# The sample stage of a two-layer hybrid decoder step: earlier first fills, scores one block later, one activation between two evictions

## The chip, the cores and the metric

The kernel runs on one core of one Trainium2 chip. The metric is the device time of one execution in microseconds (us), lower is better. A core has a TensorE (PE: matmuls, and transposes done as matmuls with the identity), a VectorE (DVE), a ScalarE (ACT), a GpSimd (POOL) and a SyncE (SP) that issues DMAs. Each engine works through its own instructions in order and waits on semaphores that the others raise. Matmuls write to PSUM, which has 8 banks of 512 fp32 per partition; DVE and ACT read it. Copying a bank to SBUF is called an eviction here.

## The reference, cut to what matters

One inference step of a prompt (512 tokens) and of 8 samples (4 tokens each, 2048 tokens of past in paged caches): one mLSTM layer, a shared K/V projection, one layer of native sparse attention. The change touches the attention of the samples alone. Per sample it computes, in fp32:

```python
sub = rows.reshape(M, 16, 2, HKV, HD)                      # raw cache rows, M = 128 blocks of 16 tokens
first  = einsum('mpchd,cpde->mche', sub, cmp_w1[:, :16])   # c = 0 keys, 1 values
second = einsum('mpchd,cpde->mche', sub, cmp_w1[:, 16:])
hid = silu(first[:-1] + second[1:] + cmp_b1)               # (127, 2, 4, 128)
out = einsum('mche,ced->mchd', hid, cmp_w2)                # compressed keys (norm + rotary) and values
p_c = softmax(q @ kc);  o_c = p_c @ vc                     # compressed branch
score = p_c summed over heads and overlapping blocks, + forced blocks; the 16 best of 33 are kept
o_s = softmax(q @ k_sel, others hidden) @ v_sel            # selected branch, over all 2048 rows with a mask
o_w = softmax(q @ k_win) @ v_win                           # window branch, 512 rows
y = g0*o_c + g1*o_s + g2*o_w
```

## The kernel before, in words

The program has six stages one after another, with barriers between them: inputs, mLSTM, projections, prompt attention, sample attention (`phase_sample`, lines 1929 to 2474) and output. Only `phase_sample` is touched. In the profile it lies from 1664 us to 2149 us.

It handles the 8 samples in a software pipeline of two. `attend(seg, n, with_next)` does the attention of sample n; between its steps PE does `products` of sample n+1, the first layer of the compression. The seven passes of the loop (`pe.Fori(0, NS - 1)`, n = 0 to 6) each hold one sample's attention and the next sample's products. Sample 0's products come ahead of the loop, and sample 7's attention comes behind it with nothing in between.

- **Fills.** Each sample takes 30 "fills", numbered 0 to 29: PE writes one bank (mostly by four transposes), and ACT or DVE evicts it. Fill j goes to bank j % 3. Fills 0 to 7 turn the cached rows for the products of c = 0 (`turn_pieces`, L2102), 8 and 9 the window keys and 11 to 18 the selected keys (`turn_keys`, L2131), 10 holds window scores, 19 to 26 turn the rows for c = 1, and 27 to 29 turn the probabilities (L2212 to L2219). `FILLS_ON_ACT` says which are evicted by ACT (0, 2, 4, 6, 8, 9, 11, ...), the others by DVE. `room(seg, j)` is PE's wait before a fill: for the eviction of fill j - 3, which had the same bank, if that is in the same run of fills; for the first three of a run it waits by another rule (line 2089).
- **Runs.** `Fills` counts a segment's fills, so that a wait can be written as a number of evictions. Inside the loop a segment is all of 0 to 29. Ahead of the loop it is 0 to 7 and 19 to 26 (two runs); for the last sample 8 to 18 and 27 to 29.
- **Products.** `products(seg, c, ks)` (L2112) is two matmuls for each block k; `fill_in(c, [k])` does them for the next sample inside `attend`. They sum in bank 3 (c = 0) and bank 7 (c = 1). `hid_mm` counts finished sums, and ACT's `silu` (L2283) reads the bank and raises `hid_ok`, for which the second layer (L2153) at the head of `attend` waits.
- **Scores.** `score(seg, 0)` and `score(seg, 1)` (L2139) multiply queries with four slots of turned keys each, so they wait for the evictions of fills 11 to 14 and 15 to 18. `oc_mm` (L2205) is the compressed branch's output, `top_in` says that DVE has read the block scores out of bank 4.
- **The other engines.** ACT's order is written out in its own `attend` and in the loop at L2326, DVE's likewise. POOL gathers the paged rows by indirect DMA and copies them to `pieces`: the selected rows of sample n+1 are asked for once `pv_mm` (L2241) of sample n is done. SP loads the window rows and, near the end, the output weights.

Inside the loop PE goes through: fills 0 to 7, second layer, block 0 of c = 0, fills 8 and 9, block 1, fill 10, blocks 2 and 3, fills 11 to 14, compressed scores (L2182), score 0, block 4, transpose of the compressed probabilities (L2187), fills 15 to 18 with small matmuls between them (L2190, L2195), score 1, blocks 5 to 7, fills 19 to 26, blocks 0 and 1 of c = 1, `oc_mm`, fills 27 to 29, blocks 2 and 3, `pv_mm`, blocks 4 to 7.

Of the kernel before, what the change touches and what calls it, by code (L numbers as in the profile page):

```python
# [16 lines left out]
ACT = mybir.ActivationFunctionType  # L17
# [5 lines left out]
TP, NS, TS_ = 512, 8, 4  # L23
# [1903 lines left out]
def phase_sample(nc, I, S):  # L1927

    with ExitStack() as ctx:
# [62 lines left out]
        def both(n):  # L1992
            return Fills(range(30), n * 30 + n_front, n * on_act + n_front // 2, n * (30 - on_act) + n_front // 2)
# [85 lines left out]
        def _(pe):  # L2079
            ident = C("ident")  # L2080

            def room(seg, j):

                if j - 3 in seg.fills:
                    if j - 3 in FILLS_ON_ACT:
                        pe.wait_ge(E["out_a"], seg.out_a(j - 3))
                    else:
                        pe.wait_ge(E["out_d"], seg.out_d(j - 3))
                elif seg is not first[0] or j >= 3:
                    pe.wait_ge(E["out_a"], seg.out_a(j - 1))  # L2090
                    pe.wait_ge(E["out_d"], seg.out_d(j - 1))

# [49 lines left out]
            def attend(seg, n, with_next):  # L2142


                def fill_in(c, ks):
                    if with_next:
                        products(seg, c, ks)
# [33 lines left out]
                for pr in range(2):  # L2181
                    t = pe.matmul(bank[strip(0, pr), 4, 0:M - 1], qz[:, pr, :], kct[:, pr, :], start=True, stop=True)  # L2182
                t.then_inc(E["cs_mm"], 1)
                score(seg, 0)
                fill_in(0, [4])
                hold(pe, E["cs_ok"], n + 1, E["pass_pe"])
# [7 lines left out]
                for half in range(2):  # L2194
                    t = pe.matmul(bank[half * R:(half + 1) * R, 4, 0:NSEL], C("same_ht"), ov[:, :], start=True, stop=True)  # L2195
                t.then_inc(E["group_mm"], 1)
                score(seg, 1)
                fill_in(0, [5, 6, 7])
                if with_next:
                    turn_pieces(seg, n + 1, 1)  # L2200
                fill_in(1, [0, 1])

                pe.wait_ge(E["top_in"], n + 1)
# [3 lines left out]
                t.then_inc(E["oc_mm"], 1)  # L2207

                hold(pe, E["exp_ok"], n * 2 + 2, E["pass_pe"])
# [53 lines left out]
        def _(act):  # L2263

            def pieces_out(seg, m, c):
                for j in (range(0, 8, 2) if c == 0 else range(19, 27, 2)):
                    act.wait_ge(E["turned"], seg.turned(j))
                    if j == 19:
                        act.wait_ge(E["hid_mm"], m * 2 + 1)
                    if j == 0 and seg is not first[0]:  # L2270
                        act.wait_ge(E["hid_mm"], m * 2)
                    out, src = xt_of(j)
                    act.copy(out, src).then_inc(E["out_a"], 1)
# [5 lines left out]

            def silu(m):  # L2280
                for c in range(2):
                    act.wait_ge(E["hid_mm"], m * 2 + c + 1)
                    act.activation(hid[:, c, :, :], bank[:, 3 if c == 0 else 7, 0:BKV * (M - 1)].rearrange("p (h m) -> p h m", h=BKV),  # L2283
                                   ACT.Silu, bias=S.b1[:, c:c + 1]).then_inc(E["hid_ok"], 1)

            def attend(seg, n, with_next):
# [23 lines left out]
                if with_next:  # L2310
                    pieces_out(seg, n + 1, 1)
                act.wait_ge(E["max_ok"], n * 2 + 2)
# [9 lines left out]

            pieces_out(first[0], 0, 0)
            pieces_out(first[0], 0, 1)
            silu(0)
            with act.Fori(0, NS - 1) as n:  # L2326
                pieces_out(both(n), n + 1, 0)
                attend(both(n), n, True)
                silu(n + 1)
            attend(last, NS - 1, False)  # L2330
# [318 lines left out]
```

## Time and profile before

| | |
|---|---|
| median of 3 runs | 2231.38 us (2228.94 to 2234.61) |
| the profiled execution's own time | 2226.32 us |
| its span, first to last instruction | 2224.7 us |
| PE busy | 2019.6 us (91% of the span) |
| DVE, ACT, POOL busy | 702.8, 473.8, 226.5 us |
| mean granted TensorE clock | 0.946 |

The profile shows one execution. A timeline row gives the start, the duration, engine, line, operation and tile of a group of instructions that follow each other, and in brackets how long the engine sat idle before it and what released it. Matmul ends are modelled and matmuls overlap, so a group's start is more certain than its end, and the time from one group's start to the next one's start says what a step really takes. PE counts each fp32 matmul twice. A row of waits sums the idle time of one line by releaser, with the number of times and the longest. A row of windows gives the busy time of each engine in a stretch, the clock granted to TensorE there (1.00 is its upper level, 2.4 GHz; 0.50 would be the lower, 1.2 GHz), and the DMA share.

### The profile page before, as it was taken

To read this page: it belongs to the slowest core of one execution; us is meant where nothing else is said; L and a number is where in the kernel's file an instruction comes from. 1 tells how busy PE (TensorE), PEld (TensorE's weight loads), DVE (VectorE), ACT (ScalarE), POOL (GpSimd) and SP (SyncE) were. 2 spreads that over 40 slices of the span, in tenths; PEclk is the share of its full clock that TensorE was granted. 3 is DMA by queue.
4 is the path that set the end of the run, shared out by engine and by line. 5 is a ranking of instruction groups with operands and counts; after the bars stand their busy time and mean duration, and the time that the engine had idled before them with its cause. 6 is when DMAs were issued, how large, how long until landed. Compare 5 with 4: busy or idle time off the path is not lost. (4 is left out here: it accounts for less than half of the span.)

```text
span 2224.7 us, 26140 instructions
## 1 busy us (share of the span) xinstructions
PE 2019.6 (91%) x9651; PEld 1177.8 (53%) x9651; DVE 702.8 (32%) x1553; ACT 473.8 (21%) x1028; POOL 226.5 (10%) x332
## 2 busy tenths in 40 slices
PE   6998999999999999978889999578869999999878
PEld 3225554664555466447754468445545555555457
DVE  2011323332332332230121340355542444444332
ACT  1110211121121112110020012244442333333310
POOL 0000010001001000100000000132332111111000
PEclk9998999999999999989999998688889999999979
DMA  6753353246134423623312164400004444443331
GB/s 177 265 202 139 134 179 143 77 167 240 48 122 173 158 77 137 229 90 127 108 44 76 42 157 147 156 2 1 1 18 192 167 163 170 170 170 141 116 94 41
DMA packets 119263, 281.31 MB, mean 126 GB/s; under 512 B 33224, under 2 KB 41870, under 8 KB 115447
## 3 DMA queue, kind: packets, MB, share of 16 engines
q1 hardware_dynamic: 101004, 170.57, 23.3%
q0 software_dynamic: 12928, 109.54, 12.2%
q10 hardware_dynamic: 5268, 0.36, 0.3%
q8 instruction: 40, 0.66, 0.1%
q14 instruction: 23, 0.19, 0.0%
HBM read 227.79 MB, written 60.86 MB: 130 GB/s over the span
## 5 line engine op out<-in xcount | busy, mean ns | idle before, releaser
L2112 PE MATMUL sample_bank<-area 128*128 128x508 f32 x512 | 232.4, 599 | 7.2 <-DVE area L2352 7.2
L1022 DVE SCALAR_TENSOR_TENSOR mlstm_cring<-mlstm_cring,mlstm_cur_old,mlstm_bank 128x512 f32<-128x512 f32 x128 | 87.1, 743 | 223.4 <-PE mlstm_bank L788 223.4
L2112 PEld LDWEIGHTS sample_bank<-area 128*128 128x128 f32 x512 | 92.6, 190 | 116.2 <-issue 106.5
L1302 PE MATMUL proj_bank<-stage,area 128*128 128x512 f32 x320 | 142.9, 605 | 6.3 <-ACT area L1379 6.3
L706 PE MATMUL mlstm_bank<-h,stage 128*128 128x272 f32 x512 | 120.7, 398 | 7.6 <-SPq L594 7.6
L761 PE MATMUL mlstm_bank<-h,stage 128*128 128x272 f32 x512 | 121.2, 395 | 0.0
L772 PE MATMUL mlstm_bank<-stage,h 128*128 128x512 f32 x256 | 114.1, 599 | 0.0
L706 PEld LDWEIGHTS mlstm_bank<-h,stage 128*128 128x128 f32 x512 | 98.5, 193 | 28.3 <-DVEq L941 7.7
L317 PE MATMUL start_bank<-stage,start_c_t 128*9 128x512 f32 x256 | 111.3, 592 | 1.8 <-DMA stage<-in_b_ada_w 0.6
L1731 PE MATMUL prompt_bank<-const,x 128*128 128x128 f32 x336 | 64.5, 337 | 52.4 <-ACT area L1802 42.7
L723 PE MATMUL mlstm_bank<-stage,h 128*128 128x512 f32 x256 | 110.9, 594 | 0.0
L761 PEld LDWEIGHTS mlstm_bank<-h,stage 128*128 128x128 f32 x512 | 96.0, 190 | 27.9 <-issue 9.1
L1302 PEld LDWEIGHTS proj_bank<-stage,area 128*128 128x128 f32 x320 | 61.1, 193 | 87.8 <-issue 86.3
L1678 POOL TENSOR_SCALAR x<-x,prompt_coef,gnat 128x128 f32<-128x128 f32 (+3 forms) x128 | 76.5, 607 | 171.8 <-DVE prompt_coef L1879 171.7
L1731 PEld LDWEIGHTS prompt_bank<-const,x 128*128 128x128 f32 x336 | 46.7, 172 | 86.7 <-POOL x L1678 64.1
L1787 ACT ACTIVATE x<-prompt_bank,prompt_nm 128x128 f32<-128x128 f32 (+3 forms) x128 | 66.3, 524 | 102.7 <-DVEq L1872 98.6
L2102 PE MATMUL sample_bank<-const,sample_pieces 128*128 128x128 f32 x512 | 68.3, 284 | 19.0 <-DVE area L2352 6.7
L2352 DVE COPY area<-sample_bank 128x512 f32<-128x512 f32 x64 | 44.2, 691 | 125.8 <-PE sample_bank L2102 125.8
L772 PEld LDWEIGHTS mlstm_bank<-stage,h 128*128 128x128 f32 x256 | 47.3, 190 | 66.0 <-issue 66.0
L723 PEld LDWEIGHTS mlstm_bank<-stage,h 128*128 128x128 f32 x256 | 48.3, 190 | 62.7 <-issue 62.7
L2102 PEld LDWEIGHTS sample_bank<-const,sample_pieces 128*128 128x128 f32 x512 | 58.4, 145 | 35.9 <-issue 20.1
L1260 PE MATMUL proj_bank<-area,stage 128*128 128x272 f32 x256 | 60.5, 400 | 17.6 <-DMA area<-act_scratch 17.6
(489 smaller groups left out, 2752.4 us busy)
## 6 DMA issues: line engine op xcount, KB each, us to landing
stage<-in_a_w_in SPq DMA_DIRECT2D x16, 2048.0 KB, 9.0
mlstm_cring<-in_state_C SPq DMA_DIRECT2D x32, 1024.0 KB, 5.4
o_Cs<-mlstm_cring POOLq DMA_DIRECT2D x32, 1024.0 KB, 4.7
stage<-in_a_ada_w SPq DMA_DIRECT2D x6, 2048.0 KB, 7.9
stage<-in_b_ada_w SPq DMA_DIRECT2D x6, 2048.0 KB, 8.0
stage<-in_kv_ada_w SPq DMA_DIRECT2D x4, 2048.0 KB, 7.9
stage<-in_a_w_out SPq DMA_DIRECT2D x4, 2048.0 KB, 10.8
sample_winr<-in_cache_kv_win SPq DMA_DIRECT2D x8, 1024.0 KB, 5.2
```

The costliest lines, as they stand in the source:

```text
L317: last = pe.matmul(bank[0:NS + 1, s, :], c_t[:, k, :], ada_w[:, s, k, :], start=(k == 0), stop=(k == KD - 1))
L706: last = pe.matmul(o[:, 0:HALF], win[:, 0, k, i * P:(i + 1) * P], S.h[:, k, at:at + HALF], start=(k == 0), stop=(k == KD - 1))
L723: last = pe.matmul(o, S.h[:, k, i * P:(i + 1) * P], win[:, 1, k, :], start=(k == 0), stop=(k == KD - 1))
L761: last = pe.matmul(o[:, 0:HALF], win[:, 0, k, i * P:(i + 1) * P], S.h[:, k, half * HALF:(half + 1) * HALF], start=(k == 0), stop=(k == KD ...
L772: last = pe.matmul(o, S.h[:, k, i * P:(i + 1) * P], win[:, 1, k, :], start=(k == 0), stop=(k == KD - 1))
L1022: dve.scalar_tensor_tensor(c, c, cur_old[:, n:n + 1], bank[:, b_big("outer", n * KH + k), :], ALU.mult, ALU.add).then_inc(E["c_new"], 1)
L1302: last = pe.matmul(o, h[:, k, a * P:(a + 1) * P], w[:, k, :], start=(k == 0), stop=(k == KD - 1))
L1678: last = pool.tensor_scalar(prob[:, u % 3, h, 0:w], prob[:, u % 3, h, 0:w], coef[:, u % 3, h:h + 1], S.gnat[:, a, at:at + 1], ALU.mult, AL ...
L1731: last = pe.transpose(out[:, b * P:(b + 1) * P], src, ident)
L1787: act.activation(prob[:, u % 3, h, 0:w], sc_bank(u, h)[:, 0:w], ACT.Exp, bias=nm[:, u % 3, h:h + 1], accum_out=den[:, u % 3, h:h + 1])
L2102: t = pe.transpose(bank[:, j % 3, q * M:(q + 1) * M], pieces[:, p % BKV, k * P:(k + 1) * P], ident)
L2112: t = pe.matmul(out, S.w1[:, c, o * 8 + k, :], xt[:, k, :, o:o + M - 1], start=(k == 0 and o == 0), stop=(k == 7 and o == 1))
```

## The change

1. `room`: the first three fills of a run no longer wait for all fills ahead of them, the run's own first ones among them, but for the fills ahead of the run.
2. PE in `attend`: block 4 of c = 0 goes ahead of score 0; block 5 goes ahead of score 1; `oc_mm` goes ahead of blocks 0 and 1 of c = 1.
3. ACT: the second `silu` (c = 1) of a sample goes from the end of a loop pass to the head of the next one, behind the eviction of fill 0 and ahead of those of fills 2, 4 and 6. After the last pass it stands alone behind the loop.

```diff
                 elif seg is not first[0] or j >= 3:
-                    pe.wait_ge(E["out_a"], seg.out_a(j - 1))
-                    pe.wait_ge(E["out_d"], seg.out_d(j - 1))
+                    run = max(f for f in seg.fills if f <= j and f - 1 not in seg.fills)
+                    pe.wait_ge(E["out_a"], seg.out_a(run - 1))
+                    pe.wait_ge(E["out_d"], seg.out_d(run - 1))
...
                 t.then_inc(E["cs_mm"], 1)
+                fill_in(0, [4])
                 score(seg, 0)
-                fill_in(0, [4])
...
                 t.then_inc(E["group_mm"], 1)
+                fill_in(0, [5])
                 score(seg, 1)
-                fill_in(0, [5, 6, 7])
+                fill_in(0, [6, 7])
                 if with_next:
                     turn_pieces(seg, n + 1, 1)
-                fill_in(1, [0, 1])
-
                 pe.wait_ge(E["top_in"], n + 1)
...
                 t.then_inc(E["oc_mm"], 1)
-
+                fill_in(1, [0, 1])
                 hold(pe, E["exp_ok"], n * 2 + 2, E["pass_pe"])
...
-            def silu(m):
-                for c in range(2):
-                    act.wait_ge(E["hid_mm"], m * 2 + c + 1)
+            def silu(m, c):
+                act.wait_ge(E["hid_mm"], m * 2 + c + 1)
...
-            pieces_out(first[0], 0, 0)
-            pieces_out(first[0], 0, 1)
-            silu(0)
+            pieces_out(first[0], 0, (0, 2, 4, 6))
+            pieces_out(first[0], 0, (19, 21, 23, 25))
+            silu(0, 0)
             with act.Fori(0, NS - 1) as n:
-                pieces_out(both(n), n + 1, 0)
+                pieces_out(both(n), n + 1, (0,))
+                silu(n, 1)
+                pieces_out(both(n), n + 1, (2, 4, 6))
                 attend(both(n), n, True)
-                silu(n + 1)
+                silu(n + 1, 0)
+            silu(NS - 1, 1)
             attend(last, NS - 1, False)
```

`pieces_out` on ACT takes its list of fills as an argument now; the lists are the old ones.

On ACT the loop's first instructions are these, as one piece of the difference (`sample_bank` is PSUM, `area` holds the turned rows, `sample_hid` the activated first layer; the semaphores carry names of an earlier stage that used the same ones: `start_x_in` is `hid_mm`, `start_const_in` is `turned`):

```order
 L2271 ISA [waits start_const_in]
 L2273 COPY area<-sample_bank 128x4x128 [waits start_x_in]
+L2281 ISA
+L2282 ACTIVATE sample_hid<-sample_bank,b 128x508 [waits start_x_in]
 L2267 REGISTER_ALU
 L2273 COPY area<-sample_bank 128x4x128 [waits start_const_in]
```

The activation stands behind the eviction of fill 0, which has its two waits as before, and ahead of that of fill 2; no table load comes with it.

On PE, around score 1 (L2139, L2140 in the changed kernel), before:

```order
L2195 MATMUL sample_bank<-x,const 64x33 x2
L2135 REGISTER_ALU
L2136 REGISTER_ALU
L2139 MATMUL sample_bank<-sample_kt,x 32x512 x4
L2112 MATMUL sample_bank<-area 128x508 x6
```

and in the changed kernel:

```order
L2196 MATMUL sample_bank<-x,const 64x33 x2
L2113 MATMUL sample_bank<-area 128x508 x2
L2136 REGISTER_ALU
L2137 REGISTER_ALU
L2140 MATMUL sample_bank<-sample_kt,x 32x512 x4
L2113 MATMUL sample_bank<-area 128x508 x4
```

One block (two matmuls) of the next sample's products moved from behind the score to ahead of it; around score 0 it is the same with block 4.

On PE, behind fills 19 to 26 (L2102, L2103 in the changed kernel), before:

```order
L2102 MATMUL sample_bank<-const,sample_pieces 128x128 x4
L2107 REGISTER_ALU
L2108 REGISTER_ALU
L2112 MATMUL sample_bank<-area 128x508 x4
L2205 MATMUL sample_bank<-x 32x128 x2
```

and in the changed kernel:

```order
L2103 MATMUL sample_bank<-const,sample_pieces 128x128 x4
L2205 MATMUL sample_bank<-x 32x128 x2
L2108 REGISTER_ALU
L2109 REGISTER_ALU
L2113 MATMUL sample_bank<-area 128x508 x4
```

The two small matmuls `oc_mm` moved ahead of the two registers that hold the blocks' wait for the evictions, and of the blocks.

## Rows read from the trace of the kernel before

**Rows 1.** The page: busy time, share of the span, instructions by engine.
```profile
PE 2019.6 (91%) x9651; PEld 1177.8 (53%) x9651; DVE 702.8 (32%) x1553; ACT 473.8 (21%) x1028; POOL 226.5 (10%) x332
```

**Rows 2.** Windows: length, busy us (and count) of PE, PEld, DVE, ACT, POOL; PEclk, DMA, GB/s.
```profile
400.00:500.00 100.00, 99.66 (x421) 63.51 (x420) 30.65 (x66) 19.89 (x41) 6.99 (x13) 1.00 0.34 123
1764.14:1819.80 55.66, 52.06 (x346) 30.32 (x345) 22.59 (x66) 17.98 (x33) 10.30 (x12) 1.00 0.42 170
2124.00:2132.00 8.00, 2.92 (x12) 2.00 (x12) 2.67 (x4) 1.89 (x4) 0.00 (x0) 0.66 0.52 99
```

**Rows 3.** Waits of PE, 1667 to 2140 us: us in total, times, longest.
```profile
PE sample_bank L2139 <- DVE sample_kt L2357: 7.9, 16, 0.6
PE sample_bank L2112 <- DVE area L2352: 7.2, 9, 0.9
PE sample_bank L2102 <- DVE area L2352: 6.7, 7, 1.0
PE sample_bank L2102 <- ACT area L2273: 6.5, 8, 0.9
```

**Rows 4.** Timeline of PE, head of the loop's second pass: fills 0 to 7.
```profile
1764.14 0.60 PE L2102 MATMUL sample_bank<-const,sample_pieces 128*128 128x128 f32 x4
1765.61 0.65 PE L2102 MATMUL sample_bank<-const,sample_pieces 128*128 128x128 f32 x4 [0.86 <-ACT area L2273]
1767.22 3.04 PE L2102 MATMUL sample_bank<-const,sample_pieces 128*128 128x128 f32 x24 [0.96 <-DVE area L2352]
1770.10 1.88 PE L2153 MATMUL sample_bank<-w,sample_hid 128*127 128x64 f32 x16
```

**Rows 5.** Timeline of ACT in the same stretch, and its eviction of fill 19.
```profile
1764.35 0.68 ACT L2283 ACTIVATE sample_hid<-sample_bank,b 128x508 f32<-128x508 f32 x1 [10.73 <-PE sample_bank L2112]
1764.97 0.58 ACT L2273 COPY area<-sample_bank 128x512 f32<-128x512 f32 x1
...
1796.59 0.58 ACT L2273 COPY area<-sample_bank 128x512 f32<-128x512 f32 x1 [7.52 <-PE sample_bank L2102]
```

**Rows 6.** Timeline of PE, same pass: both scores, fills 19 to 26, `oc_mm`.
```profile
1782.54 0.41 PE L2182 MATMUL sample_bank<-x 128*32 128x127 f32 x4
1783.39 1.07 PE L2139 MATMUL sample_bank<-sample_kt,x 128*32 128x512 f32 x8 [0.44 <-DVE sample_kt L2357]
...
1786.29 0.32 PE L2187 MATMUL sample_bank<-const,x 64*127 64x64 f32 x1
...
1788.81 0.31 PE L2195 MATMUL sample_bank<-x,const 64*64 64x33 f32 x4
1789.67 1.07 PE L2139 MATMUL sample_bank<-sample_kt,x 128*32 128x512 f32 x8 [0.55 <-DVE sample_kt L2357]
...
1795.88 3.96 PE L2102 MATMUL sample_bank<-const,sample_pieces 128*128 128x128 f32 x32
1800.63 3.67 PE L2112 MATMUL sample_bank<-area 128*128 128x508 f32 x8 [0.78 <-DVE area L2352]
1804.23 0.41 PE L2205 MATMUL sample_bank<-x 127*32 127x128 f32 x4
```

**Rows 7.** Timeline of DVE, same pass: the step that releases L2187.
```profile
1785.56 0.28 DVE L2391 TENSOR_SCALAR x<-x,sample_denc 64x127 f32<-64x127 f32 x1
```

**Rows 8.** Timeline of PE ahead of the loop: fill 19, and the blocks behind fill 26.
```profile
1688.15 0.60 PE L2102 MATMUL sample_bank<-const,sample_pieces 128*128 128x128 f32 x4
...
1694.73 1.52 PE L2112 MATMUL sample_bank<-area 128*128 128x508 f32 x3 [0.87 <-DVE area L2352]
```

**Rows 9.** Timeline of PE, last sample: fills 28 and 29.
```profile
2129.29 1.12 PE L2219 MATMUL sample_bank<-const,x 128*128 128x128 f32 x4 [0.72 <-ACT x L2317]
2131.28 1.09 PE L2219 MATMUL sample_bank<-const,x 128*128 128x128 f32 x4 [0.87 <-DVE x L2424]
```

**Rows 10.** Timeline of POOL: selected rows asked for; DMA issues: median us to landing.
```profile
1813.88 0.96 POOL L1578 DMA_INDIRECT sample_sel<-in_cache_kv_sel,sample_sblk  x1 [39.20 <-PE sample_bank L2241]
...
sample_sel<-in_cache_kv_sel,sample_sblk POOLq DMA_INDIRECT x8, 14.4
```

More of the change, by code:

```diff
@@ L2263, in _, with pieces_out @@
         def _(act):
-            def pieces_out(seg, m, c):
-                for j in (range(0, 8, 2) if c == 0 else range(19, 27, 2)):
+            def pieces_out(seg, m, fills):
+                for j in fills:
                     act.wait_ge(E["turned"], seg.turned(j))
@@ L2278, in keys_out @@
                 act.copy(out, src).then_inc(E["out_a"], 1)
-            def silu(m):
-                for c in range(2):
-                    act.wait_ge(E["hid_mm"], m * 2 + c + 1)
-                    act.activation(hid[:, c, :, :], bank[:, 3 if c == 0 else 7, 0:BKV * (M - 1)].rearrange("p (h m) -> p h m", h=BKV),
-                                   ACT.Silu, bias=S.b1[:, c:c + 1]).then_inc(E["hid_ok"], 1)
+            def silu(m, c):
+                act.wait_ge(E["hid_mm"], m * 2 + c + 1)
+                act.activation(hid[:, c, :, :], bank[:, 3 if c == 0 else 7, 0:BKV * (M - 1)].rearrange("p (h m) -> p h m", h=BKV),
+                               ACT.Silu, bias=S.b1[:, c:c + 1]).then_inc(E["hid_ok"], 1)
             def attend(seg, n, with_next):
@@ L2310, in attend @@
                 if with_next:
-                    pieces_out(seg, n + 1, 1)
+                    pieces_out(seg, n + 1, (19, 21, 23, 25))
                 act.wait_ge(E["max_ok"], n * 2 + 2)
```

## The prediction
> **What bounds the kernel now.** I read the page first: PE is busy 2019.6 of 2224.7 us [rows 1], so only time that PE loses can be won. The windows then say what the stage in question looks like: one loop pass is 55.7 us, PE is busy for 52.06 of it, ACT for 18 and DVE for 22.6, the DMAs for 0.42, and TensorE's clock is granted in full, 1.00 [rows 2]. So in the loop PE is the bound, and the remaining 3.6 us of a pass are its waits. The list of PE's waits names them: 6.7 and 6.5 us ahead of fills (L2102), 7.9 us ahead of scores (L2139), 7.2 us ahead of blocks (L2112), all for an eviction by DVE or ACT [rows 3]. The times are seven or eight (sixteen for the two scores) with the longest hardly above the mean: the same short waits in each pass. The timelines show where they lie, and the change aims at each of them.
>
> **The first fills of a pass (change 1 with 3).** Fill 0 starts at 1764.14. Fill 1 waits until ACT has evicted fill 0 (idle 0.86), fill 2 until DVE has evicted fill 1 (idle 0.96); the six from fill 2 on then run through, and the second layer starts at 1770.10 [rows 4]. That is 5.96 us from start to start. The bank of fill 1 was free all the while. With the new rule fills 0, 1 and 2 follow each other, and what eight fills then take is shown by fills 19 to 26, which have no such wait today: 3.96 us, or about 3.8 to the next start, since a group's start lies 0.1 to 0.2 ahead of the modelled end of the one before (1770.10 against 1767.22 + 3.04 = 1770.26) [rows 4, 6].
>
> ACT must keep that pace. Today it does the activation (0.68 us from 1764.35) and then evicts fill 0 at 1764.97 [rows 5]. In the run of fills 19 to 26 the first eviction starts 0.71 us after the first fill (1795.88 to 1796.59) [rows 5, 6], so fill 0's should start at 1764.85 and end at 1765.43, and the activation follows until 1766.1. Fill 2, ready at about 1765.7, is then evicted until 1766.7, and fill 5, which needs that bank, starts some 2.6 us behind fill 0, where the undisturbed pace (3.8/8 for each fill, five of them) puts it at 2.4 to 2.5. I charge 0.1. The second layer needs the activation 3.9 us behind fill 0, at 1768.0; it is done by 1766.1, so the moved activation has 1.9 us of cover. The gain is 5.96 - 3.9 = **2.05 us** a pass. Bounds: if the whole activation stood on the path, 2.15 - 0.68 = 1.5; without any disturbance 2.15.
>
> **Score 0 behind block 4.** From the compressed scores (1782.54) to the transpose L2187 (1786.29) PE takes 3.75 us with 0.44 idle [rows 6]. The two stay, the block covers DVE's last eviction, and the idle goes, with about 0.1 that a start after a wait loses by not overlapping. But L2187 itself waits for DVE's scaling, which ends at 1785.84 [rows 7], and PE would now come at 1786.29 - 0.52 = 1785.77. A release takes about 0.06, as from the end of fill 0's eviction (1764.97 + 0.58) to fill 1 (1765.61) [rows 4, 5], so some 0.13 of a new wait comes in. The gain is **0.4 us**; bounds 0.2 (a longer chain on DVE) and 0.52. Nothing else needs score 0 early: ACT's and DVE's next evictions wait for fills 15 and 16, which stand behind L2187.
>
> **Score 1 behind block 5.** The score starts at 1789.67, 0.86 us after the group of small matmuls at 1788.81, which occupies PE for some 0.25 of that [rows 6]. The gain is **0.6 us**. The score is 1.2 us later against the stream. DVE adds the mask to it after a chain that ends just then, so up to 0.1 us may pass to DVE, and the exponential behind it stands on ACT behind fill 25's eviction, microseconds later. Bounds 0.4 and 0.65.
>
> **`oc_mm` ahead of the blocks.** After fill 26 PE waits 0.78 us for DVE's eviction. `oc_mm` takes 0.41 us and needs none of it [rows 6]; as its first or last part overlaps with its neighbours, **0.35 us** of the wait is covered; bounds 0.2 and 0.41. DVE gets its input earlier.
>
> **Ahead of the loop and behind it.** For sample 0, fills 19 to 26 form a run of their own, and the blocks start 1694.73 - 1688.15 = 6.58 us after fill 19 [rows 8]. In the loop the same piece takes 1800.63 - 1795.88 = 4.75 [rows 6]. The gain is **1.8 us**. In the last sample fills 28 and 29 lose their waits of 0.72 and 0.87 [rows 9]; with 0.15 for each restart, **1.9 us**. Its other parts gain nothing: there are no blocks to put ahead of the scores, and fill 9's shorter wait ends in the wait for the selected rows. In that stretch the granted clock is 0.66 [rows 2], a mixture of both levels after a longer wait.
>
> The Trainium skill (TensorE: Matmul & The Clock Gate, section "HAM oscillation — how this bites in real kernels") says that idle gaps send the array back to half its clock and that closing them keeps it warm. In the loop the trace shows no such loss, 1.00 with all its gaps [rows 2], so by rows there is nothing more to gain there; in the last sample the rule would add something, which I leave to the range.
>
> **Sum.** A pass gains 2.05 + 0.4 + 0.6 + 0.35 = 3.4 us; seven give 23.8. With 1.8 and 1.9 it is **27.5 us**. The profiled execution has 2224.7 of span in 2226.3 us of its own time, so 2198.8. It lies 5 us below the median of the runs shown, 2231.4; taken from that, **2204 us**. By the lower bounds a pass gives 1.5 + 0.2 + 0.4 + 0.2 = 2.3, together 16 + 3 = 19; by the upper ones 2.15 + 0.52 + 0.65 + 0.41 = 3.7, together 26 + 4 = 30. So 2201 to 2212 by the terms.
>
> **Rivals.** *The activation in the way:* if ACT, not PE, sets the pace of fills 2 to 7 (activation and later evictions fully on the path, and one more eviction late), a pass wins 1.0 instead of 2.05 there, together 20 us: 2211. Against it stands that ACT is idle for most of those microseconds; for it, that the four evictions and the activation are 3.0 us of work in a 3.8 us run.
>
> *The selected rows become the bound:* they are asked for when `pv_mm` ends, at 1813.88, and land 14.4 us later, at 1828.3 [rows 10]; the first to want them is fill 11 of the next pass. Fills 11 to 14 end with the compressed scores (1782.54), and four fills take 1.9 us at the pace of fills 19 to 26, so it starts at 1780.6 and one pass later at 1836.3 [rows 6]. Of the 8 us between, only what the first fills gain, 2, is used up. Were the landing over 8 us later, as other DMAs could make it, PE would wait for DMA and the gain be nil: 2231.
>
> *A lower clock:* with PE's gaps filled, its granted clock could fall in the loop. A pass of 52.3 us of work takes 52.3/c; with the 3.7 us at both ends the change breaks even near c = 0.93 and is slower by 0.3% below about 0.915. At 0.9 it would be 58.1 us a pass, 7 x 2.4 - 3.7 = 13 us slower: 2244. Against it: the low clock of the last sample, 0.66, goes with a PE that is busy for 2.9 of 8 us, while a stretch with PE busy for 99.66 of 100 us has 1.00 [rows 2].
>
> *It doesn't do what it says:* the new waits could still contain the run's own evictions. In the loop a segment is all of 0 to 29, so a run starts at 0 and the counts are those ahead of it; I see no such case.
>
> **How the numbers follow.** The forecast has 0.8, the activation in the way 0.13, the rows as the bound 0.04, the lower clock 0.03. The first two are faster by over 0.3%, about what a measurement of this kernel can tell from no change: faster 0.93, same 0.04, slower 0.03. The range takes the terms' bounds, 2201 to 2212, and the 2 to 3 us by which single runs stand off their median: 2198 to 2214. That holds the second case too.
>
> **What would show it.** In the timeline after, fills 0 to 7 of a pass should stand as one group of 32 matmuls in about 4 us, with the activation on ACT between the evictions of fills 0 and 2. The 13 us of waits ahead of L2102 and the 7.9 ahead of the scores should be nearly gone, a wait of about 0.1 ahead of L2187 may be new, the wait ahead of the blocks should be 0.4 a pass, and a pass should take 52.3 us at a clock of 1.00. If fill 5 or 6 waits for ACT by over 0.5 us, the first rival is right; if fill 11 waits for DMA, the second; a clock under 0.95 in the loop, the third. The prediction would be wrong if a wait of a microsecond turned up in a step that has none today.

## The result, and the profile after

| | before | after |
|---|---|---|
| median, compared on one chip | 2230.45 us (5 runs) | 2198.66 us (5 runs, 2192.2 to 2200.36) |
| ratio | | 0.9851, 95% interval 0.9834 to 0.9868 |
| the profiled execution's own time | 2226.32 us | 2198.66 us |
| its span | 2224.7 us | 2197.0 us |

The change is faster by 1.5%, some 33 us by the ratio. The forecast was 2204 with a range from 2198 to 2214; the median after lies at the range's lower end, and the ratio times the median of before, 2197.2, a little below it. The direction and the mechanism were right and the gain was too small. Between the two profiled executions lie 27.7 us, which is what the prediction's terms gave, 27.5. Most of what follows is about the 5 us between these two ways of counting.

The busy line of the page after, beside [rows 1]:

```profile
PE 2016.3 (92%) x9651; PEld 1179.6 (54%) x9651; DVE 703.5 (32%) x1553; ACT 473.4 (22%) x1028; POOL 227.8 (10%) x332
```

The work is the same, and PE's busy time fell by 3.3 us at an unchanged number of instructions. The window over one loop pass (length, busy time and count of PE, PEld, DVE, ACT, POOL, granted clock, DMA share, GB/s), beside the second of [rows 2]:

```profile
1760.55:1812.99 52.44, 51.86 (x347) 30.32 (x345) 22.69 (x66) 17.86 (x33) 10.38 (x12) 1.00 0.45 182
```

A pass takes 52.44 instead of 55.76 us, with PE busy for 51.86 of it. PE's waits in the whole stretch, beside [rows 3]:

```profile
PE sample_bank L2103 <- POOL sample_pieces L2043: 5.0, 1, 5.0
PE sample_bank L2113 <- DVE area L2354: 4.8, 9, 0.9
...
PE sample_bank L2132 <- DMA sample_sel<-in_cache_kv_sel,sample_sblk: 3.5, 1, 3.5
...
PE sample_bank L2140 <- DVE sample_kt L2359: 0.9, 2, 0.6
...
PE sample_bank L2188 <- DVE x L2393: 0.3, 1, 0.3
PE sample_bank L2103 <- ACT area L2273: 0.2, 1, 0.2
```

The 6.7 and 6.5 us ahead of the first fills have become 0.2, once. The 7.9 us ahead of the scores have become 0.9, twice, both in the last sample where no block covers them. Ahead of the blocks 4.8 us are left, 0.44 in each pass and 0.9 twice ahead of the loop. The 5.0 us for POOL were there before, ahead of sample 0, and so was the wait of 3.5 us for the last sample's selected rows (3.2 us in the profiled execution of before).

PE's timeline of the same pass (start, duration, instruction, and in brackets the idle time before it with its releaser), beside [rows 4, 6]:

```profile
1760.55 4.04 PE L2103 MATMUL sample_bank<-const,sample_pieces 128*128 128x128 f32 x32
1764.43 1.88 PE L2154 MATMUL sample_bank<-w,sample_hid 128*127 128x64 f32 x16
...
1776.87 0.41 PE L2183 MATMUL sample_bank<-x 128*32 128x127 f32 x4
1777.21 1.97 PE L2113 MATMUL sample_bank<-area 128*128 128x508 f32 x4
1779.11 1.07 PE L2140 MATMUL sample_bank<-sample_kt,x 128*32 128x512 f32 x8
1780.31 0.29 PE L2188 MATMUL sample_bank<-const,x 64*127 64x64 f32 x1
...
1789.45 3.97 PE L2103 MATMUL sample_bank<-const,sample_pieces 128*128 128x128 f32 x32
1793.35 0.41 PE L2205 MATMUL sample_bank<-x 127*32 127x128 f32 x4
1794.20 3.67 PE L2113 MATMUL sample_bank<-area 128*128 128x508 f32 x8 [0.44 <-DVE area L2354]
1797.71 0.38 PE L2212 MATMUL sample_bank<-const,x 128*128 128x128 f32 x2
```

Fills 0 to 7 are one group of 32 matmuls and lead to the second layer in 3.88 us instead of 5.96. ACT in the same stretch, beside [rows 5], has the activation between the evictions of fills 0 and 2, and it catches up at once:

```profile
1761.35 0.59 ACT L2273 COPY area<-sample_bank 128x512 f32<-128x512 f32 x1 [11.32 <-PE sample_bank L2103]
1761.83 0.69 ACT L2282 ACTIVATE sample_hid<-sample_bank,b 128x508 f32<-128x508 f32 x1
1762.41 0.59 ACT L2273 COPY area<-sample_bank 128x512 f32<-128x512 f32 x1
1763.23 0.59 ACT L2273 COPY area<-sample_bank 128x512 f32<-128x512 f32 x1 [0.24 <-PE sample_bank L2103]
```

### The profile page after: what moved, and what is told of

It is laid out like the page before. It is cut to its first block and busy times, and to the rows that moved or that the text cites. A ratio compares the mean times of both kernels' runs of the same rounds, so it can differ in the third digit from the quotient of the medians.

```text
span 2197.0 us, 26140 instructions
## 1 busy us (share of the span) xinstructions
PE 2016.3 (92%) x9651; PEld 1179.6 (54%) x9651; DVE 703.5 (32%) x1553; ACT 473.4 (22%) x1028; POOL 227.8 (10%) x332
## 5 line engine op out<-in xcount | busy, mean ns | idle before, releaser
L2273 ACT COPY area<-sample_bank 128x512 f32<-128x512 f32 x64 | 37.6, 587 | 167.3 <-PE sample_bank L2103 167.2
L2103 PE MATMUL sample_bank<-const,sample_pieces 128*128 128x128 f32 x512 | 66.2, 284 | 5.1 <-POOL sample_pieces L2043 5.0
```

The source lines that it names most:

```text
L2103: t = pe.transpose(bank[:, j % 3, q * M:(q + 1) * M], pieces[:, p % BKV, k * P:(k + 1) * P], ident)
```

## Experiments: what each part of the change is worth

**Change 1 alone** (the new rule of `room`, everything else as before):

```diff
-                    pe.wait_ge(E["out_a"], seg.out_a(j - 1))
-                    pe.wait_ge(E["out_d"], seg.out_d(j - 1))
+                    run = max(f for f in seg.fills if f <= j and f - 1 not in seg.fills)
+                    pe.wait_ge(E["out_a"], seg.out_a(run - 1))
+                    pe.wait_ge(E["out_d"], seg.out_d(run - 1))
```

> The kernel before with the new wait ahead of the first fills alone (activation, scores and oc_mm as before). Theory 'terms': 7 x 2.05 in the passes, 1.8 ahead of the loop and 1.9 in the last sample, 18 us less what the activation ahead of fill 0's eviction costs. By the rows of before that eviction starts 0.83 us after fill 0 with the activation ahead of it, and 0.80 without in the changed kernel, so the activation costs nothing here: 2212 us, ratio 0.992, a pass of 53.8. Rival 'activation in the way' (the first fills gain only because the activation moved too): a pass of 54.3 or more, 2216 us, ratio 0.9935.

Measured: 2206.23 us, ratio 0.9889, interval 0.9865 to 0.9914. A pass takes 53.67 us, so the first fills give 55.72 - 53.67 = 2.05 us, as predicted. But the whole gain of 25 us (by the interval 19 to 30) is more than 7 x 2.05 + 1.8 + 1.9 = 18, and that is where the missing microseconds first showed.

**The change without it** (the old rule of `room` put back into the changed kernel):

```diff
-                    run = max(f for f in seg.fills if f <= j and f - 1 not in seg.fills)
-                    pe.wait_ge(E["out_a"], seg.out_a(run - 1))
-                    pe.wait_ge(E["out_d"], seg.out_d(run - 1))
+                    pe.wait_ge(E["out_a"], seg.out_a(j - 1))
+                    pe.wait_ge(E["out_d"], seg.out_d(j - 1))
```

> The changed kernel with the old wait ahead of the first fills. Theory 'clock': a pass without a dip takes 52.43 + 2.05 = 54.5 us less what the moved activation gives to fill 0's eviction there (up to 0.6), so 53.9 to 54.5, some passes 1.4 to 1.5 more with the clock at 0.50 behind the waits, and the median is 2198 + 7 x 1.5 to 2.05 + 1.8 + 1.9 + 3 to 6 for dips = 2215 to 2222, with the scatter of before. Rival 'other stages': 2212 to 2216 and no pass at a lower clock.

Measured: 2216.57 us, ratio 0.9942, interval 0.9921 to 0.9962. A pass takes 54.48 us, so scores and `oc_mm` give 55.73 - 54.48 = 1.25 us of it. Seven passes give 8.8 us, within the 8 to 18 us that the interval allows.

**The change with both activations at the end of a pass:**

```diff
             silu(0, 0)
+            silu(0, 1)
             with act.Fori(0, NS - 1) as n:
-                pieces_out(both(n), n + 1, (0,))
-                silu(n, 1)
-                pieces_out(both(n), n + 1, (2, 4, 6))
+                pieces_out(both(n), n + 1, (0, 2, 4, 6))
                 attend(both(n), n, True)
                 silu(n + 1, 0)
-            silu(NS - 1, 1)
+                silu(n + 1, 1)
```

> The changed kernel with both activations at the end of a pass again, as before. Theory 'terms': the moved activation is worth at most 0.1 us a pass either way: 2198 us, ratio 0.9875 like the changed kernel's, a pass of 52.3 to 52.5. Rival 'activation in the way': fill 3 waits for it, a pass is 52.9 to 53.1 and the time 4 us above the changed kernel's.

Measured: 2197.53 us, ratio 0.9852, interval 0.9824 to 0.9879, the same as with the move. ACT's timeline at the head of a pass in this kernel:

```profile
1759.80 0.69 ACT L2282 ACTIVATE sample_hid<-sample_bank,b 128x508 f32<-128x508 f32 x1 [10.72 <-PE sample_bank L2113]
1760.42 1.28 ACT L2273 COPY area<-sample_bank 128x512 f32<-128x512 f32 x2
```

PE's timeline there:

```profile
1759.60 4.06 PE L2103 MATMUL sample_bank<-const,sample_pieces 128*128 128x128 f32 x32
1763.50 1.88 PE L2154 MATMUL sample_bank<-w,sample_hid 128*127 128x64 f32 x16
```

The activation goes first and the evictions of fills 0 and 2 follow it without a gap. Fill 0's starts 0.82 us behind its fill, against 0.80 with the move; PE takes 3.90 us for the fills here and 3.88 there. The moved activation is worth nothing that can be measured.

## Experiments: where the other microseconds come from

**Both kernels again,** without an edit, to see more than one trace of each:

> The kernel before, unchanged, as a second trace and a null measurement. Theory 'terms' (the sum of the waits is the whole gain, 27 to 28 us, and the 31.8 us between the medians is scatter of other stages): the sample stage, from its first fill to the output stage's first matmul, takes 483.8 us again (within 1), a pass 55.7 us, and runs scatter by some 5 us with stages other than the sample stage; ratio 1.000 +- 0.002. Rival 'quick profile' (the profiled run of before was a lucky one in the sample stage, the usual one loses more there): the stage takes 487 to 490 us in this trace.

> The changed kernel, unchanged, measured again. Theory 'terms': the sample stage takes 456.5 us (within 1), a pass 52.4, and the ratio comes nearer to 1 - 27.5/2230.5 = 0.9877 than the 0.9851 measured first: 0.986 to 0.989. Rival 'quick profile': 0.985 again.

> The kernel before once more, for a third trace of it. Theory 'clock': passes take either 55.7 or 57.2 us, the long ones with a stretch at clock 0.50 right behind the two waits of the first fills, and the sample stage is 483.8 us plus about 1.46 for each long pass. Rival 'other stages': all passes 55.7, and what the time is above 2226 lies elsewhere.

> The kernel before for a fourth trace. Theory 'clock': the six passes from the first second-layer product on sum to 334.4 us with no long pass, or 338.7 with three; the stretch behind fill 29 takes 18.0 to 18.9. Rival 'other stages': 334.4.

> The changed kernel for a third trace of its own. Theory 'clock': six passes of 52.43 without exception; the stretch behind fill 29 takes 15.1 to 15.4 in most traces, at times 18.0. Rival 'other stages': a pass of 53.9 turns up here too.

Measured: before 2231.78 us (12 runs, 2223.03 to 2236.88, ratio 0.9999, interval 0.9982 to 1.0015) and single runs of 2231.42 and 2231.30; after 2197.91 (5 runs, ratio 0.9844, interval 0.9820 to 0.9868) and a single run of 2197.07. The gain is again more than the terms allow. The stage itself, from its first fill to the output stage's first matmul, takes 483.8 us in the profiled execution of before and 489.0, 490.1 and 488.8 in the three further traces, as the rival of the first expectation had it: the profiled execution was a quick one there. Of after it takes 456.5, 454.5 and 453.6. The means lie 33.1 us apart, which is the measured gain. Ahead of the stage either kernel scatters as well: the first fill starts between 1660.8 and 1671.7 us in all the traces of this document.

The traces of before differ among themselves. Here is PE at the heads of four passes of one that ran for 2231.30 us, each from fill 2 on:

```profile
1712.27 3.03 PE L2102 MATMUL sample_bank<-const,sample_pieces 128*128 128x128 f32 x24 [0.96 <-DVE area L2352]
1715.14 1.88 PE L2153 MATMUL sample_bank<-w,sample_hid 128*127 128x64 f32 x16
...
1768.03 4.50 PE L2102 MATMUL sample_bank<-const,sample_pieces 128*128 128x128 f32 x24 [0.96 <-DVE area L2352]
1772.32 1.93 PE L2153 MATMUL sample_bank<-w,sample_hid 128*127 128x64 f32 x16
...
1825.23 3.04 PE L2102 MATMUL sample_bank<-const,sample_pieces 128*128 128x128 f32 x24 [0.96 <-DVE area L2352]
1828.10 1.88 PE L2153 MATMUL sample_bank<-w,sample_hid 128*127 128x64 f32 x16
...
1880.96 4.50 PE L2102 MATMUL sample_bank<-const,sample_pieces 128*128 128x128 f32 x24 [0.96 <-DVE area L2352]
1885.30 1.88 PE L2153 MATMUL sample_bank<-w,sample_hid 128*127 128x64 f32 x16
```

The waits are those of [rows 4] in each pass, but in every second one the same 24 matmuls take 4.50 us instead of 3.04. From one second layer to the next it is 57.18, 55.78 and 57.20 us. The windows of the same trace say what happened:

```profile
1764.95:1768.03 3.08, 1.26 (x10) 0.79 (x8) 0.69 (x1) 1.21 (x2) 0.80 (x1) 1.00 1.03 447
1768.03:1769.00 0.97, 0.97 (x9) 0.97 (x10) 0.00 (x0) 0.29 (x1) 0.24 (x1) 0.99 0.94 405
1769.00:1772.00 3.00, 3.00 (x17) 3.00 (x15) 1.38 (x2) 1.18 (x3) 2.05 (x2) 0.50 1.04 448
...
1825.23:1828.10 2.87, 2.87 (x24) 2.63 (x25) 1.39 (x2) 1.41 (x3) 1.85 (x3) 1.00 0.87 377
```

In the two waits the clock is 1.00, and here it stays there for the first microsecond of the matmuls behind them; in the other two long passes of this trace it falls 0.67 and 0.40 us behind the second wait, and in another trace as little as 0.02. Then it is 0.50, the lower level, for some three microseconds in which PE has no gap, and the next pass with the same waits has none of it. Three of six such passes are long, by 1.46 us each, in this trace and in two more of unedited before; the profiled execution of before has none. The trace of the changed kernel with the old rule has the waits, too, and no long pass; its expectation had wanted some. So the waits do not always cost this. In three traces of the changed kernel, and in that of the one with both activations at the end, every pass is 52.4 us, and no trace of any kernel with the new rule, nine in all, has a long pass.

The Trainium skill (TensorE: Matmul & The Clock Gate, section "A second HAM failure mode: psum-queue depth-cycling") tells of an array that idles briefly between groups of matmuls while it cycles through PSUM banks, and whose clock goes back and forth between its two levels for it. This trace agrees, with 0.50 behind two waits of 0.86 and 0.96 us for evictions of PSUM banks. It was the section to weigh ahead of the result.

**The gaps filled, the path unchanged.** The next two kernels are the one before with transposes of the identity into an unused bank, whose result nobody reads; the output is as before. The first fills the waits behind fills 0 and 1 of a pass, the second also those ahead of fills 28 and 29 in the last sample. No fill starts earlier for it.

```diff
                     t.then_inc(E["turned"], 1)
+                    if j in (0, 1) and seg is not first[0]:
+                        for _ in range(6 + j):
+                            pe.transpose(bank[:, 5, 0:P], ident, ident)
...
                 for j in (28, 29):
+                    if not with_next:
+                        for _ in range(j - 25):
+                            pe.transpose(bank[:, 5, 0:P], ident, ident)
                     room(seg, j)
```

> The kernel before, waits and all, with useless transposes (identity into bank 5, six behind fill 0 and seven behind fill 1) that keep PE at work while it waits for the two evictions at the head of a pass. Nothing is won for the path: a pass cannot get shorter than 55.7 us. Theory 'clock' (in some passes the two waits make the granted clock fall to 0.50 for the next stretch, which costs 1.46 us each time, as three of seven passes of the second trace of before show, 57.2 against 55.7; the profiled run of before had none): every pass takes 55.7 to 55.9, no stretch at 0.50 inside the loop, and the median lies 3 to 6 us below that of before, 2226 to 2228, ratio 0.9975 to 0.9985, with less scatter. Rival 'other stages' (the scatter of before has nothing to do with the heads of the passes): the ratio is 1.000 or above, and the scatter stays.

> The kernel before with useless transposes in both places where the new wait closes gaps: behind fills 0 and 1 of each pass (as in filled_waits) and, in the last sample, three ahead of fill 28's wait and four ahead of fill 29's. The path is as long as before; only PE's gaps are filled. Theory 'clock': no pass longer than 55.8; in the last sample, from the window products behind fill 29 to the output stage's first matmul, 15.1 to 15.4 us as in three of four traces with the new wait, against 18.0 to 18.9 in all five with the old one; median 2224 to 2227, ratio 0.997 to 0.9985. Rival 'other stages': that stretch stays at 18.0 to 18.9, the median at 2229 or above.

> The same kernel for a second trace. Theory 'clock': again no pass at 57.2, and the stretch behind fill 29 at 15.1 to 15.4. Rival: either of them as in the kernel before.

Measured: the first 2227.57 us, ratio 0.9994, interval 0.9982 to 1.0006, which decides nothing; the second 2225.97 us (12 runs, against 2231.23 from 17 runs of before), ratio 0.9977, interval 0.9963 to 0.9990, and a single run of 2222.47. PE at the head of a pass in the latter:

```profile
1761.90 0.60 PE L2102 MATMUL sample_bank<-const,sample_pieces 128*128 128x128 f32 x4
1762.34 0.82 PE L2106 MATMUL sample_bank<-const 128*128 128x128 f32 x6
1763.36 0.66 PE L2102 MATMUL sample_bank<-const,sample_pieces 128*128 128x128 f32 x4 [0.21 <-ACT area L2279]
1763.85 0.93 PE L2106 MATMUL sample_bank<-const 128*128 128x128 f32 x7
1764.98 3.04 PE L2102 MATMUL sample_bank<-const,sample_pieces 128*128 128x128 f32 x24 [0.20 <-DVE area L2358]
1767.85 1.88 PE L2156 MATMUL sample_bank<-w,sample_hid 128*127 128x64 f32 x16
```

The head takes 5.95 us from start to start, as before, since the useless transposes lie in the waits. In none of three traces of these two kernels is a pass longer than 55.8 us. With the idle waits four of six traces have three long passes each (five of before, one of them with an edit behind the loop that is told below, and one of the changed kernel with the old rule); with the waits filled or gone none of twelve has one. That the low stretches come from the gaps rests on this count.

The times agree less well. The second kernel, in which work that brings no instruction forward fills the gaps, is faster by 2 to 8 us. The first has the same edit in the passes, and its interval goes from 4.0 us faster to 1.3 slower: three long passes in every run, 4.4 us or 0.2%, lie just outside of it, and what the traces of before suggest on average, three such passes in three runs of four or 3.3 us, inside. One wait takes some of the gain back: in two of the three traces of these kernels PE waits 5.8 and 6.3 us for the last sample's selected rows, against 3.0 in the third and 3.1 to 3.7 in the five traces of before. Whether the edit has to do with it is open; the kernel with change 1 alone, which has no useless work, waits 5.1 us there.

**The last sample.** From the window products behind fill 29 to the first matmul of the output stage it takes 18.0 to 18.9 us in all nine traces with the old waits, and with the new rule 15.1 to 15.4 in five of seven and 18.0 and 18.1 in the two others, the profiled execution of after among them. To see whether that is the clock, 22 useless transposes were put into the wait of 4.47 us ahead of fill 27, in either kernel, and in a third one 16 more into the wait of 2.35 us ahead of the stage's last transposes (L2258 in the changed kernel):

```diff
+                if not with_next:
+                    for _ in range(22):
+                        pe.transpose(bank[:, 3, 0:P], ident, ident)
                 hold(pe, E["exp_ok"], n * 2 + 2, E["pass_pe"])
...
+            for _ in range(16):
+                pe.transpose(bank[:, 3, 0:P], ident, ident)
             hold(pe, E["o2_ok"], NS + 1, E["pass_pe"])
```

> The kernel before with the same 22 transposes; its waits ahead of fills 28 and 29 stay. Theory that these two waits hold the clock down: the stretch from the window products to the output matmul takes 18.0 us or more, as in all traces with the old wait, though fill 27 starts at full clock. Rival, that the clock's level behind the long wait alone decides: it takes what it takes in the changed kernel with the same transposes, within 0.5 us.

> The changed kernel with 22 useless transposes ahead of fill 27 of the last sample, in the wait of 4.47 us for ACT's exponential that stands there; the output is as before. If the tail of the last sample (from fill 27 to the output matmul) is long because the granted clock is low behind that wait, fills 27 to 29 should run at the pace of the loop, 1.6 us instead of 2.7, and the stretch from the window products to the output matmul should take about 15 us or less instead of 15.1 to 18.0. If something else makes it long, 18 us remain possible and nothing moves but the start of fill 27, by up to 0.3 us.

> The changed kernel with the 22 transposes and 16 more in the wait of 2.35 us ahead of the last transposes of the stage (L2258). By the theory of the clock these 32 matmuls take 3.5 us instead of 5.6 to 7.1, and the stretch from the window products to the output matmul about 12.7 us; the last sample is 4 to 7 us shorter than in the changed kernel, the time 2193, ratio 0.9825 to the kernel before. If the clock is not what makes the tail long, 2198.

Measured: single runs of 2224.07 and 2195.32 us; the third 2197.72 us, ratio 0.9862, interval 0.9833 to 0.9892, in a comparison whose runs of before had a median of 2227.12. The stretch takes 18.03, 15.10 and 13.17 us. The first kernel's windows, from the useless work to the products:

```profile
2122.60:2125.20 2.60, 2.60 (x25) 2.38 (x22) 2.38 (x5) 0.00 (x0) 0.00 (x0) 1.00 1.05 200
2127.19:2128.50 1.31, 0.63 (x4) 0.33 (x4) 0.00 (x0) 0.62 (x2) 0.00 (x0) 1.00 0.00 0
2128.50:2131.60 3.10, 1.82 (x12) 1.20 (x12) 0.90 (x3) 0.59 (x1) 0.00 (x0) 0.80 0.00 0
2131.60:2137.30 5.70, 5.66 (x88) 3.98 (x88) 1.81 (x13) 0.21 (x1) 0.00 (x0) 0.51 0.01 3
```

Its timeline of PE has the selected branch's products and the last transposes:

```profile
2133.21 3.64 PE L2241 MATMUL sample_bank<-sample_sel,x 128*32 128x128 f32 x64
...
2139.71 6.27 PE L2261 MATMUL sample_bank<-const,x 128*128 128x64 f32 x32 [2.35 <-DVE x L2474]
```

The same two groups in the second kernel, ahead of them its fills 28 and 29:

```profile
2102.34 1.91 PE L2222 MATMUL sample_bank<-const,x 128*128 128x128 f32 x8
...
2106.21 1.96 PE L2241 MATMUL sample_bank<-sample_sel,x 128*32 128x128 f32 x64
...
2110.85 5.54 PE L2261 MATMUL sample_bank<-const,x 128*128 128x64 f32 x32 [2.35 <-DVE x L2476]
```

And in the third, with the useless transposes between them:

```profile
2107.45 1.96 PE L2241 MATMUL sample_bank<-sample_sel,x 128*32 128x128 f32 x64
...
2109.68 1.97 PE L2259 MATMUL sample_bank<-const 128*128 128x128 f32 x16
2112.12 3.75 PE L2263 MATMUL sample_bank<-const,x 128*128 128x64 f32 x32 [0.48 <-DVE x L2478]
```

That the length of this stretch is a matter of the clock is shown: the same 32 transposes take 3.75 us behind a filled wait and 5.5 to 7.1 behind an idle one. Which part the two short waits ahead of fills 28 and 29 have in it is not settled. For them speaks the pair with the same warm start. With the waits the clock falls from 1.00 to 0.51 behind them and the products take 3.64 us; without them it falls as well, but earlier (fills 28 and 29 take 1.91 us for what takes 1.04 in the loop), and it is back for the products, 1.96 us. Against them speaks that with these waits filled the stretch was still 18.1 us in both traces. Nor is a gain in time shown: 2197.72 us with its interval is not distinguishable from the changed kernel, and it is the figure (2198) that the expectation gave for the case that the clock is not the cause, though the stretch itself is shorter, 13.17 us where 12.7 was expected.

**Two kernels that go further.** In the changed kernel the window probabilities are ready long before the selected ones, so their transposes can stand ahead of blocks 0 and 1 of c = 1 and cover the 0.44 us left there; and the output weights, which arrive beside the last sample's selected rows, can be asked for once those have landed:

```diff
+            sp.wait_ge(E["sel_in"], NS * 16)
...
-                fill_in(1, [0, 1])
-                hold(pe, E["exp_ok"], n * 2 + 2, E["pass_pe"])
+                hold(pe, E["exp_ok"], n * 2 + 1, E["pass_pe"])
                 room(seg, 27)
...
+                fill_in(1, [0, 1])
+                hold(pe, E["exp_ok"], n * 2 + 2, E["pass_pe"])
```

> The changed kernel with two more edits: the three transposes of the window's probabilities go ahead of blocks 0 and 1 of c = 1, where PE waits 0.44 us a pass, and the output weights are asked for only when the last sample's selected rows have landed, which then come without that load beside them. By the rows: 0.35 x 7 = 2.5 us in the passes (52.1 each), and up to 3.5 us in the last sample, where PE waits 3.50 us for those rows: 2193 us. Rival: the rows' landing time of 19 us in the last sample is not due to the weights; then 2196.

Measured: 2190.85 us, ratio 0.9829, interval 0.9809 to 0.9849. A pass takes 52.1 us, the waits ahead of the blocks are down to 1.8 us, all of it outside of the loop, and PE no longer waits for the selected rows of the last sample (3.5 us in the profiled execution of after). The stage takes 449.6 us, against 453.6 to 456.5 in the traces of after. The interval of the time overlaps that of the change itself (0.9834 to 0.9868), so the gain over it is read from the trace alone. The second adds useless transposes in the two waits at the end, as above, 18 and 16 of them:

> The kernel with the window probabilities ahead of the blocks and the output weights asked for later (2190.85 us), with 18 useless transposes ahead of the transposes of the new tokens' probabilities and 16 ahead of L2258. By the theory of the clock 4 to 6 us shorter: 2186, ratio 0.980. If the clock is not what makes the tail long, 2191.

Measured: 2189.27 us, ratio 0.9825, interval 0.9795 to 0.9856. It has the lowest median of all, but it can't be told from the one without them.

## Why the prediction was right, and where it was not

Point by point, in us, by starts of groups in the profiled executions:

| step | predicted | measured |
|---|---|---|
| fills 0 to 7, a pass | 2.05 | 5.96 - 3.88 = 2.08 |
| score 0, from L2182 to the transpose behind block 4 | 0.4 | 3.75 - 3.44 = 0.31 |
| score 1, from that transpose to fill 19 | 0.6 | 9.59 - 9.14 = 0.45 |
| `oc_mm`, from fill 19 to fill 27 | 0.35 | 8.69 - 8.26 = 0.43 |
| a pass | 3.4 | 55.73 - 52.43 = 3.30 |
| sample 0's blocks behind fill 26 | 1.8 | 6.58 - 4.69 = 1.89 |
| fills 28 and 29 of the last sample | 1.9 | 5.60 - 3.52 = 2.08 |

The first pass's own head gives a little less (1.83), since one fill there waits 0.16 us for ACT. All seven passes, the piece ahead of them and the last fills come to 26.9 us where the sum had 27.5. So the terms were right, each to within 0.2 us, and in part by errors that cancel. Score 0 gave less than its 0.4: L2188 starts 1.20 us behind the score, where the block behind score 1 starts 0.99 us behind that, so 0.2 us are lost there, where the prediction charged 0.13 for a new wait for DVE. `oc_mm` gave a little more than its upper bound of 0.41. And 3.88 us for the first fills is the 3.9 that the prediction took, but not for its reason: fills 19 to 26, with no activation among their evictions, take 1793.35 - 1789.45 = 3.90 us to the next start and not 3.8, and the activation, which was charged 0.1, costs nothing that can be measured. The rivals fell each at the sign that the text gave for it: no fill 5 or 6 waits for ACT, fill 11 waits for no DMA in the loop (in the last sample it does, as before), and the clock in the loop is 1.00.

**The step that failed is the last one of the sum:** "It lies 5 us below the median of the runs shown, 2231.4; taken from that, 2204 us." The difference between the profiled execution and the median was taken for scatter that the changed kernel would have as well. It isn't. In four of five traces of before with nothing changed in its passes (one with the warm start) three of six passes are 1.46 us longer, 4.4 us together, and the profiled execution happened to have none. The change takes away the waits behind which that happens, so the 4.4 us go with them. In the prediction's terms, the loss to the clock stood at nothing in the sum and was 4.4 us in most traces. The sum against the profiled execution's own time, 2198.8, stood in the text one sentence earlier and is what the profiled execution after took, 2198.66. That it agrees to 0.1 us is luck: the stage is 27.4 us shorter, but it starts 1.4 us later, and what comes behind it is 1.7 us shorter.

What led there is the sentence "In the loop the trace shows no such loss, 1.00 with all its gaps [rows 2], so by rows there is nothing more to gain there", which made of one trace a statement on the kernel, and the clause after it, "which I leave to the range", for the last sample: the range that followed, 2201 to 2212 by the terms, has no term for it. In the traces the last sample's tail gives another 2 us on average (18.2 over the nine traces with the old waits, 16.0 over the seven with the new rule), and from 18.0 to 15.1 it is 3. The terms, 26.9, the long passes, 3.3 on average of the four unedited traces of before, and this tail make up 32 of the 33 us measured. The long passes are shown to come from the gaps; of the tail it is shown that the clock makes it and open why.

A range that took both into its upper bound of the gain, 30 + 4.4 + 3, would have reached down to 2194 (2231.4 - 37.4).

## What to carry to other kernels

A wait on the engine that bounds the kernel can cost more than its idle time: look at how long the same group of matmuls takes behind it, in each pass, and at the granted clock there. Where the one trace at hand lies below the median of the runs, ask what the slower runs may do that this trace doesn't show, and whether the change removes it, before the difference is carried over to the forecast. An operation moved to relieve an engine that already has slack (the activation here) brings nothing.

## What the runs showed of the hardware

Two waits of 0.86 and 0.96 us, with 0.65 us of work between them and steady work on either side, are followed by some three microseconds at half the clock in every second pass of four traces, and by none in two others. The clock falls only after the second wait has ended, by up to a microsecond (0.96, 0.67 and 0.40 us in the trace shown), while PE is busy without a gap.

The Trainium skill (TensorE: Matmul & The Clock Gate, section "What's actually happening") says that the watch on the array's activity runs free of the program, so that one kernel meets it at another phase in each run. The alternation of 57.2 and 55.8 us, the fall that moves from 0.96 to 0.40 us behind the wait within one trace, and the traces with none agree with it; no run here shows the watch itself.

Transposes whose result nobody reads, put into a wait of 2.35 us, kept the clock at 1.00 for the 32 transposes behind it, which took 3.75 us. With the wait left idle the clock was at half by 1.7 us behind it at the latest, and they took 5.5 to 7.1.
